# Windowed-attention layers: keys projected by token tile first, then the first quad's queries, the values and the first scores

## The reference, cut to what matters

```python
def mixer_a(x, w_qkv, b_qkv, sinks, w_o, b_o, cos, sin):
    """Sliding-window (128) grouped-query attention with per-head sinks."""
    qkv = x @ w_qkv + b_qkv
    q = apply_rope(qkv[..., :nq].reshape(B, S, A_HEADS, HEAD_DIM), cos, sin)
    k = apply_rope(qkv[..., nq:nq + nkv].reshape(B, S, A_KV_HEADS, HEAD_DIM), cos, sin)
    v = qkv[..., nq + nkv:].reshape(B, S, A_KV_HEADS, HEAD_DIM)
    o, _ = block_attention(q, k, v, WIN_BLK, A_WINDOW - 1, True, sinks)
    return o.reshape(B, S, nq).astype(x.dtype) @ w_o + b_o

for i in range(DEPTH_2):                       # kinds 0, 1, 2, 0
    ...
    x = layer_norm(DN_ALPHA * x + h, ln_g[i, 0], ln_b[i, 0])
    x = layer_norm(DN_ALPHA * x + swiglu(x, w_gate_up[i], w_down[i]), ln_g[i, 1], ln_b[i, 1])
```

## Time and profile before

| | us |
|---|---|
| Median of 3 runs | 2326.47 (2325.89 to 2328.65) |
| Profiled execution, its own time | 2323.77 |
| Its span | 2322.0 |
| PE busy | 2149.4 (93% of the span) |
| DVE busy | 1280.7 (55%) |
| ACT busy | 919.2 (40%) |
| POOL busy | 109.0 (5%) |
| Mean granted clock of PE | 0.958 |

### The profile page before, as it was taken

The page is one execution under the profiler, slowest core; times in us unless marked ns, Lnnn a source line. Parts: engine busy times, 40 slices in busy tenths (PEclk is TensorE's granted clock), DMA queues, the critical chain, the costliest instruction groups (busy, mean ns, idle before and its releaser), DMA issues.

```text
span 2322.0 us, 27972 instructions
## 1 busy us (share of the span) xinstructions
PE 2149.4 (93%) x11510; PEld 1732.2 (75%) x11510; DVE 1280.7 (55%) x1903; ACT 919.2 (40%) x1448; POOL 109.0 (5%) x115
## 2 busy tenths in 40 slices
PE   4998999998999998899999998999998999988997
PEld 1556867775788877688799887788787788766886
DVE  1263742325555566555568676655576755656554
ACT  1123432003444435344345544444355444354442
POOL 1000000000000001000001012100001000020000
PEclk8799989998999999999999999999999999989999
DMA  7213334533454542345544332455543554424551
GB/s 291 85 66 152 122 140 147 194 137 117 162 181 181 182 164 108 136 181 183 173 182 171 128 126 93 145 183 182 179 146 128 181 181 181 163 94 152 181 181 73
DMA packets 47102, 357.23 MB, mean 154 GB/s; under 512 B 5370, under 2 KB 5557, under 8 KB 9664
## 3 DMA queue, kind: packets, MB, share of 16 engines
q1 hardware_dynamic: 41616, 334.51, 40.0%
q0 software_dynamic: 4784, 18.38, 2.3%
q10 hardware_dynamic: 576, 2.55, 0.3%
HBM read 354.38 MB, written 1.05 MB: 153 GB/s over the span
## 4 chain that ended last, share of the span: by engine, by line
PE 83%; DVE 10%; ACT 3%; issue 2%; DMA 1%; POOL 0%; ACTq 0%; DVEq 0%
PE pg L435 53%; PE pd L435 23%; PE pm L435 4%; DMA rh<-in_ctx 1%; PE pm L866 1%; DVE low L1592 1%; DVE small L1889 1%; DVE rs L1925 1%; DVE rs L1924 1%; DVE rs L1885 1%; DVE ar L2101 1%; DVE ar L1683 1%; ACT ar L1483 1%; PE pm L1008 1%; DVE xs L1935 0%
## 5 line engine op out<-in xcount | busy, mean ns | idle before, releaser
L1592 DVE TENSOR_TENSOR low<-ring,high 128x1024 fp32r<-128x1024 f32 x512 | 622.9, 1236 | 356.9 <-ACT high L1143 356.7
L435 PE MATMUL pg<-high,xs 128*128 128x512 f32 (+1 forms) x2496 | 749.6, 378 | 29.5 <-DVE xs L1935 14.3
L1143 ACT CAST high<-ring 128x1024 fp32r<-128x1024 f32 x512 | 525.1, 1048 | 372.7 <-PE pd L435 163.9
L435 PEld LDWEIGHTS pg<-high,xs 128*128 128x128 f32 x2496 | 464.2, 194 | 118.3 <-issue 21.3
L435 PE MATMUL pg<-low,xs 128*128 128x512 f32 (+1 forms) x1248 | 467.5, 375 | 0.0
L435 PE MATMUL pd<-high,hid 128*128 128x512 f32 x960 | 311.7, 396 | 7.0 <-DVE hid L2016 7.0
L435 PEld LDWEIGHTS pg<-low,xs 128*128 128x128 f32 x1248 | 242.5, 194 | 40.7
L435 PE MATMUL pg<-xs,high 128*128 128x256 f32 x1344 | 242.1, 283 | 0.0
L435 PEld LDWEIGHTS pd<-high,hid 128*128 128x128 f32 x960 | 180.7, 188 | 50.5 <-DVE hid L2016 8.2
L435 PEld LDWEIGHTS pg<-xs,high 128*128 128x128 f32 x1344 | 206.3, 188 | 5.0 <-issue 4.7
L435 PE MATMUL pg<-rh,ring 128*128 128x256 f32 (+1 forms) x832 | 207.4, 409 | 0.0
(11 more groups left out here) (322 smaller groups left out, 2048.9 us busy)
## 6 DMA issues: line engine op xcount, KB each, us to landing
ring<-in_wstream SPq DMA_DIRECT2D x256, 1024.0 KB, 4.8
ring<-in_wstream SPq DMA_DIRECT2D x31, 2048.0 KB, 7.8
gb<-in_long_rows POOLq DMA_DIRECT2D x21, 512.0 KB, 4.3
hdec<-in_hy_decay POOLq DMA_DIRECT2D x4, 512.0 KB, 4.4
rh<-in_xt ACTq DMA_DIRECT2D x1, 1024.0 KB, 23.1
rh<-in_ctx ACTq DMA_DIRECT2D x1, 1024.0 KB, 27.9
cx<-in_cx_tables POOLq DMA_DIRECT2D x1, 1024.0 KB, 5.1
cx<-in_dft_tables POOLq DMA_DIRECT2D x1, 1024.0 KB, 8.5
```

The source lines that it names most:

```text
L435: ins = nc.tensor.matmul(dst, lhs, rhs, start=start, stop=stop, skip_group_check=skip)
L1143: nc.scalar.copy(high[:, (s - split0) % NHIGH, :], ring[:, s % NRAW, :]).then_inc(S("high_done"), 1)
L1592: V.tensor_tensor(low[:, s % NRAW, :], ring[:, s % NRAW, :], high[:, (s - split0) % NHIGH, :].bitcast(F32), ALU.subtract).then_inc(S("low_ ...
```

## The change

Four orders are rewritten alike for layers 0 and 3 (the weight stream, PE, ACT, DVE): keys, first quad's queries, values, first scores, instead of values, keys, first queries, second queries, first scores. The keys take over the place across the two token tiles: `project` gets a branch in which each tile's tokens are streamed alone, 48 products of 128 columns for tile 0, the second `turn`, and 48 products of 128 columns for tile 1. `project_values` runs its two halves without a wait between them there.

```diff
-            parts = [(part, 2 * g + i) for g in range(groups) for part in "vkq" for i in range(2)]
+            parts = [(part, 2 * g + i) for g in range(groups) for part in ("kqv" if kind == 0 else "vkq") for i in range(2)]
...
-                opening = q % 4 == 0 and g == 0
+                opening = q % 4 == 0 and kind > 0 and g == 0
...
             def project(part, q, g):
 
                 dst = bank(part, q, g, "proj_out", JOB[part, q, g] + 1)
+                layer = q // 4
+                opening = KINDS[layer] == 0 and part == "k"
+                if opening:
+                    turn(2 + 2 * layer, 0)
                 w = pair_of_units()
+                if opening:
+                    for t in range(TT):
+                        if t:
+                            turn(2 + 2 * layer, 1)
+                        pe.wait_ge(S("x_ready"), 4 * (1 + 2 * layer) + 2 * t + 2)
+                        for m in range(2):
+                            for k in range(KT):
+                                for i, (l, r) in enumerate(((0, 0), (0, 1), (1, 0))):
+                                    last = mm(dst[:, m * T + t * P:m * T + (t + 1) * P], w[l][:, m, k * P:(k + 1) * P],
+                                              xs[:, r, k, t * P:(t + 1) * P], k == 0 and i == 0, k == KT - 1 and i == 2)
+                    last.then_inc(S("unit_used"), 2)
+                    return
...
-                    project_values(q0, 0)
                     project("k", q0, 0)
                     project("q", q0, 0)
+                    project_values(q0, 0)
+                    score(q0, 0)
                     project("q", q0 + 1, 0)
-                    score(q0, 0)
                     project("q", q0 + 2, 0)
...
-                    take("v", q0, 0)
                     take("k", q0, 0)
                     take("q", q0, 0)
+                    take("v", q0, 0)
                     take("q", q0 + 1, 0)
...
-                    rotate("v", q0, 0)
                     rotate("k", q0, 0)
                     rotate("q", q0, 0)
+                    rotate("v", q0, 0)
+                    mask(q0, 0)
                     rotate("q", q0 + 1, 0)
-                    mask(q0, 0)
```

## The result

| | before | after |
|---|---|---|
| Median | 2327.39 us (2325.89 to 2328.65, 4 runs) | 2355.53 us (2351.80 to 2361.34, 4 runs) |
| Ratio after / before | | 1.0123, 95% interval 1.0099 to 1.0148 |
| Profiled execution's span | 2322.0 | 2356.2 |
| Mean granted clock of PE | 0.958 | 0.946 |

The change makes the kernel 28 us slower, where +5 was forecast. The sign was right, the size was not, and the time lies outside the range of 2325 to 2352. The nearest of the rivals is the first, a clock that stays at half through the keys, priced at 2348 to 2352.

What follows compares the result with a forecast made beforehand. PE was taken to bound the kernel, with 83% of the chain of waits. Layer 0's +2.9 (+6.9 on PE, less 4.1 idle ACT) and layer 3's +2.1 made +5.0: 2331.5 us median, range 2325 to 2352.

Steps and rivals of the forecast that it cites:

- a clock that stays at half through the keys: First rival: PE's clock stays at half through the opening keys, +8.4 us a layer, 2348 to 2352 in all; chance 0.18.
- The order and its chain: First scores before second queries remove ACT's 4.1 us idle per layer; the third scores' wait falls from 4.33 to 2.2.
- the sum for the head: Opening to third scores: +6.9 us on PE less 4.1 of idle ACT, +2.9 in layer 0, +1.4 to +2.9 in layer 3.
- the doubled job: Opening keys as 96 products of 128 columns instead of 48 of 256: 48 x 0.120 = +5.7 us in each layer.
- The price of a 128-column product: In the opening keys, 128 columns cost what their weight load costs, 0.112 to 0.120 us; 0.120 was taken.
- 32 at 0.120 take 3.8, so tile 0 ends at 864.7: Layer 0's first-tile keys: after 16 half-clock products taking 3.4 us, the other 32 run at full clock.
- Tile 1: 5.7: Layer 0's second-tile keys: 48 products at 0.120 us, from the go-ahead at 867.4 to 873.1.
- Layer 3 was forecast at +2.1: Layer 3's delay: +2.9 if half clock behind the second transposes is paid again, +1.4 if avoided; middle taken.
- the rival: The half clock through the keys, +8.4 us a layer; chance 0.18.
- the one-column run at 355: Profile row set against the half-clock rival: one-column products at 355 kept clock 1.00 for 3.6 us.
- the 16-column rows at 105: Profile row given for the half-clock rival: products of few columns ran back to back 5 us at 0.50 without its rising.
- Behind that I count nothing: After the third scores: no further cost, as later exponents follow `mask` and the queries' moves, both 2.9 us later.

Runs made afterwards that it cites:

- wide: The changed kernel with the keys' 96 opening products streaming 256 columns instead of 128, on the same weight loads: 2335.64 us, ratio 1.0048 to before.
- narrow: The kernel before with the first quad's queries in layers 0 and 3 made with 96 products of 128 columns instead of 48 of 256: 2338.21 us, ratio 1.0063.
- after2: The changed kernel unaltered, run again for a second trace: 2353.22 us.
- keysonly: The changed kernel with jobs reordered to keys, values, first queries, second queries, first scores, keeping the 128-column keys: 2360.33 us, ratio 1.0130 to before.
- before2: The kernel before unaltered, run again for a second trace: 2326.98 us.
- whole: The changed kernel with the keys not cut by tile, both transposes first, then 48 products of 256 columns: 2328.13 us, ratio 1.0021 to before.
- narrow2: The kernel of narrow unaltered, run once more for a second trace: 2344.96 us.

## Why the prediction was wrong, step by step

**The order and its chain: right.** ACT's idle 3.84 + 0.25 went, and the third scores wait 1.86 where 2.2 was predicted. Where the clock rises as the prediction had it, the sum for the head holds: wide gives +3.0 and +1.5 in the heads for +2.9 and +1.4 to 2.9. That it fits to a tenth is in part luck, since before's own heads differ by 3.4, and wide's whole time is +11 and not +5. narrow gives the doubled job +5.1 for +5.7 (the product costs 0.112, not the 0.120 taken).

**The price of a 128-column product: right at full clock.** It costs what its weight load costs, as the one-column rows said, and not half of 0.120. The Trainium skill's 81 ns for 128 columns ("TensorE: Matmul & The Clock Gate", section "Back-to-back issue gap") does not hold for these operands, whose measured pace is 112 ns.

**The step that failed: "32 at 0.120 take 3.8, so tile 0 ends at 864.7", and "Tile 1: 5.7" behind it.** I took the clock's rise at 861 from the kernel before, where 256-column products had brought it about, and gave it to 128-column products. They do not bring it about: in six openings (after, after2 and keysonly, two layers each) the clock was at half from at most 2.4 us after the start to the last key. That term was mis-sized by this much: in layer 0 tile 0 took 8.1 instead of 7.2, tile 1 10.3 instead of 5.7, and the job behind the keys, the first queries, began at half clock as well, 4.5 us of it, some 2 us lost. With 0.7 for slower transposes and the way of tile 1 (3.33 instead of 2.66) this is 8.2, and the head is 11.0 longer than in the first trace of before, 8.1 more than the 2.9 forecast. Layer 3 was forecast at +2.1, the middle between a clock that rises, falls again behind the second transposes and rises once more, and one that rises and stays. It did not rise at all: tile 0 took 10.1, and the head is 11.3 longer than in that trace, 9 more than forecast.

**Why the rival got too little.** Its price was nearly right, +8.4 a layer, and its place too. The row that I set against it, the one-column run at 355 that kept 1.00, shows a clock that does not fall; narrow confirms just this for 128 columns. The question was whether a fallen clock rises, and for that the 16-column rows at 105 were the evidence: they ran for 5 us without a gap and it did not. I weighed a row on keeping against a case of raising.

**What the forecast left out: the tails.** "Behind that I count nothing" missed the 2.8 us more that PE waits for the copies of turned weights, and above all that a tail takes 57.2 to 62.2 us by where the clock falls. Two traces each give 58.0 on average for before and 60.5 for after. So 21.7 of the heads and about 5 of the tails make 27 of the 30 us by which the mean of after's two spans (2356.2, 2351.4) exceeds that of before's (2322.0, 2325.2); the other 3 lie outside these tails and heads. Whether the change makes long tails likelier, or two traces are too few, stays open.

## What to carry to other kernels

Cutting a product to fill a wait can cost twice: the weight loads double, and where the load sets the pace, as here (0.112 for 128 columns, 0.120 for 256), each half costs nearly what the whole did; and behind a wait the emptier products may not bring the clock back. Idling and running 256-column products afterwards was some 24 us cheaper here. To judge such a cut, ask of the rows for what *raised* the clock in the place, not for what kept it.

When a chain through ACT sets the end, take out of it what depends on nothing: moving a table load of 1.28 us took 1.4 us off a wait of PE, and with it the runs could tell a gain (0.9956) that they could not tell for the order alone.

## What the runs showed of the hardware

- Behind a wait, 128-column fp32r products with a load each did not bring a fallen clock back: in six openings they ran at half clock for 16 to 21 us, broken only by the transposes and 1.4 us of wait between the tiles. The same 96 with 256 columns were at full clock 3.4 and 4.4 us after the first (wide), and other 256-column products after 3.3 to 6.1 us (before, before2, whole). The same 128-column products kept a full clock for 10.8 us four times (narrow, narrow2). The Trainium skill, "TensorE: Matmul & The Clock Gate", section "Why this matters for your kernels", advises to keep TensorE busy continuously for the full rate; these traces agree for products of 256 columns only.
- A 128-column fp32r product with a fresh 128x128 load starts every 0.112 us at full clock and every 0.213 at half; a 256-column one every 0.120 and 0.213. At half clock the two cost the same.
- A part of the run-to-run spread of this kernel has a place: tails of 57.2, 58.8, 60.4 or 62.2 us, by how long the clock is at half around the bias products. Differences below 0.2% need many runs; 12 against 24 did not settle 3 us.
